# Which units of layer 0's MLP carry a modulation block's sums and transposes

## The reference

```python
def modulation(cvec, w, b):
    m = jax.nn.silu(cvec) @ w + b
    return jnp.split(m[..., None, :], 6, axis=-1)

def sq_relu_mlp(h, w1, w2):
    return jnp.square(jax.nn.relu(h @ w1)) @ w2

for i in range(DEPTH_2):
    sh1, sc1, g1, sh2, sc2, g2 = modulation(c, w_mod[i], b_mod[i])
    csh1, csc1, cg1, csh2, csc2, cg2 = modulation(c_ctx, w_mod[i], b_mod[i])
    ...
    x = sublayer_residual(x, sq_relu_mlp(x * (1.0 + sc2) + sh2, mlp_w1[i], mlp_w2[i]), g2, ln_g[i, 1], ln_b[i, 1])
    if not last:
        ...
        xc = sublayer_residual(xc, sq_relu_mlp(xc * (1.0 + csc2) + csh2, mlp_w1[i], mlp_w2[i]), cg2, ln_g[i, 1], ln_b[i, 1])
```

## Time and profile before

| what | value |
|---|---|
| median of 3 runs | 1266.71 us (1266.68 to 1266.92) |
| the profiled execution | 1269.88 us |
| its span, first to last instruction | 1268.1 us |
| mean granted clock of PE | 0.996 |
| PE busy | 1237.6 us, 98% |
| DVE busy | 886.8 us, 70% |
| ACT busy | 571.9 us, 45% |
| DMA | 218.44 MB, mean 172 GB/s |
| chain that ended last | PE 86%, DVE 4%, ACT 4%, DMA 3% |

### The profile page before, as it was taken

The page is one execution under the profiler, slowest core; times in us unless marked ns, Lnnn a source line. Parts: engine busy times, 40 slices in busy tenths (PEclk is TensorE's granted clock), DMA queues, the critical chain, the costliest instruction groups (busy, mean ns, idle before and its releaser), DMA issues.

```text
span 1268.1 us, 23901 instructions
## 1 busy us (share of the span) xinstructions
PE 1237.6 (98%) x10201; PEld 1150.3 (91%) x10201; DVE 886.8 (70%) x1381; ACT 571.9 (45%) x894; POOL 97.5 (8%) x144
## 2 busy tenths in 40 slices
PE   7999999999999999999999999999999999899997
PEld 4899999999988788999998998998999779899997
DVE  4667765677664675678686787786887987767656
ACT  4443346645774454545413313223155665634531
POOL 0111112100001111000000011111100000000000
PEclk9999999999999999999999999999999999999998
DMA  9997898546344554222545456576444203555550
GB/s 353 393 305 242 269 251 198 158 159 196 97 159 159 183 178 155 101 74 93 167 151 166 126 174 196 175 244 199 133 134 155 79 2 131 169 199 180 187 167 34
DMA packets 170283, 218.44 MB, mean 172 GB/s; under 512 B 6224, under 2 KB 147993, under 8 KB 170042
## 3 DMA queue, kind: packets, MB, share of 16 engines
q1 hardware_dynamic: 140328, 148.18, 35.6%
q0 software_dynamic: 29152, 67.42, 17.5%
q10 hardware_dynamic: 698, 1.32, 0.3%
HBM read 215.77 MB, written 1.12 MB: 171 GB/s over the span
## 4 chain that ended last, share of the span: by engine, by line
PE 86%; DVE 4%; ACT 4%; DMA 3%; issue 2%; SPq 1%; POOL 0%; DVEq 0%; ACTq 0%
PE bank L1401 31%; PE bank L723 13%; PE bank L742 10%; PE bank L775 7%; PE bank L758 4%; PE bank L1295 2%; PE bank L1368 1%; DMA raw<-in_w_in 1%; PE bank L1382 1%; PE bank L833 1%; SPq L570 1%; PE bank L1558 1%; ACT whi L1630 1%; PE bank L1496 1%; DMA pre<-in_w_ada 1%
## 5 line engine op out<-in xcount | busy, mean ns | idle before, releaser
L2251 DVE TENSOR_TENSOR wlo<-raw,whi 128x2048 fp32r<-128x2048 f32 x131 | 297.3, 2274 | 87.5 <-ACT whi L1630 87.1
L1630 ACT ACTIVATE whi<-raw 128x2048 fp32r<-128x2048 f32 x131 | 247.9, 1899 | 182.5 <-PE bank L1401 129.6
L1401 PE MATMUL bank<-a_lo,whi 128*128 128x256 f32 (+1 forms) x656 | 159.4, 314 | 0.0
L1401 PE MATMUL bank<-whi,m_hi 128*128 128x256 f32 x528 | 148.0, 280 | 0.0
L1401 PE MATMUL bank<-whi,m_lo 128*128 128x256 f32 x528 | 147.7, 280 | 0.0
L1401 PE MATMUL bank<-wlo,m_hi 128*128 128x256 f32 x528 | 147.7, 280 | 0.0
L1401 PEld LDWEIGHTS bank<-a_lo,whi 128*128 128x128 f32 x656 | 107.0, 188 | 8.8
L723 PE MATMUL bank<-h_hi,whi 128*128 128x256 f32 x368 | 104.2, 283 | 0.0
L723 PE MATMUL bank<-h_lo,whi 128*128 128x256 f32 x368 | 102.5, 278 | 0.0
L723 PE MATMUL bank<-h_hi,wlo 128*128 128x256 f32 x368 | 102.4, 278 | 0.0
L1401 PEld LDWEIGHTS bank<-whi,m_lo 128*128 128x128 f32 x528 | 100.3, 190 | 0.0
(11 more groups left out here) (476 smaller groups left out, 3314.3 us busy)
## 6 DMA issues: line engine op xcount, KB each, us to landing
raw<-in_mlp_w SPq DMA_DIRECT2D x64, 1024.0 KB, 5.2
raw<-in_w_in SPq DMA_DIRECT2D x32, 1024.0 KB, 7.7
graw_b<-in_w_mod POOLq DMA_DIRECT2D x64, 512.0 KB, 5.1
raw<-in_ev_w_in SPq DMA_DIRECT2D x12, 1024.0 KB, 5.1
pre<-in_w_ada SPq DMA_DIRECT2D x16, 512.0 KB, 9.7
graw_a<-in_w_mod POOLq DMA_DIRECT2D x16, 512.0 KB, 6.8
Y<-in_w_mod POOLq DMA_DIRECT2D x16, 512.0 KB, 4.1
raw<-in_od_w_qkv SPq DMA_DIRECT2D x6, 1024.0 KB, 4.8
```

Source lines behind the costliest of these rows:

```text
L1401: mm = nc.tensor.matmul(o, x, y, start=(k == 0 and i == 0), stop=(k == KT - 1 and i == 2))
L1630: nc.scalar.activation(split_pair(u, kt * cols)[0], landing(u, kt * cols), ACT.Copy).then_inc(hi_done, 1)
L2251: nc.vector.tensor_tensor(split_pair(u, n)[1], landing(u, n), bf(whi[u % HI], n), ALU.subtract).then_inc(lo_done, 1)
```

## The change

Two tables in the kernel's plan are edited. In round 1, the quarters of the units j = 0 to 7 go from 1, 1, 1, 0, 2, 1, 2, 2 to 2, 2, 2, 0, 1, 1, 1, 1; the sum stays ten. Block 19 is turned after unit (1,0) instead of (1,1), block 20 after (1,2) instead of (1,5). Block 21, the fourth, is still turned after (1,7), and its four quarters are in one slot each. Nothing else is changed.

```diff
--- before.py
+++ after.py
@@ -422,13 +422,13 @@
         GY_BANK = (7, 0, 7, 6)
         KV_OUT = 10
         U_Q, B_LOOP, LRING = 72, 18, 3
-        LOOP_N = [[0, 0, 0, 0, 1, 1, 2, 2], [1, 1, 1, 0, 2, 1, 2, 2], [3, 2, 1, 1, 3, 3, 3, 3], [3, 2, 1, 1, 2, 2, 2, 0]]
+        LOOP_N = [[0, 0, 0, 0, 1, 1, 2, 2], [2, 2, 2, 0, 1, 1, 1, 1], [3, 2, 1, 1, 3, 3, 3, 3], [3, 2, 1, 1, 2, 2, 2, 0]]
         LOOP_Q, n_ = {}, 0
         for r_ in range(4):
             for j_ in range(8):
                 LOOP_Q[r_, j_] = range(n_, n_ + LOOP_N[r_][j_])
                 n_ += LOOP_N[r_][j_]
-        REDUCE = {(0, 6): 18, (1, 1): 19, (1, 5): 20, (1, 7): 21, (2, 2): 22, (2, 4): 23, (2, 6): 24, (2, 7): 25,
+        REDUCE = {(0, 6): 18, (1, 0): 19, (1, 2): 20, (1, 7): 21, (2, 2): 22, (2, 4): 23, (2, 6): 24, (2, 7): 25,
                   (3, 1): 26, (3, 2): 27, (3, 5): 28, (3, 7): 29}
         LN_CALL = [0, 2, 4, 5]
         LN_T0 = [24, 32, 40, 48, 56]
```

## The result

| | before | changed |
|---|---|---|
| median, 8 runs each | 1266.91 us (1266.01 to 1270.23) | 1270.38 us (1269.71 to 1271.80) |
| ratio of the medians | | 1.0028, 95% interval 1.0019 to 1.0037 |
| the profiled execution | 1269.88 us | 1271.80 us |
| its span | 1268.1 us | 1270.0 us |
| PE busy | 1237.6 us | 1237.1 us |

The account below looks back on a forecast made before the run. PE, busy for 98% of the span, was taken to bound the kernel. A wait of +2.6, a clock fall of +1.7 and closer spacing of -1.1 gave +3.2 us on 1266.7: 1269.9 us, range 1267.8 to 1271.8.

Parts of the forecast that it names:

- the wait: Behind (1,2), PE waits for DVE's sums before block 20's transposes: 2.6 us, bounds 0.5 and 3.5.
- the spacing: Closer matmuls in (1,1), (1,6) and (1,7): 0.2 + 0.9 = 1.1 us gained; other bound 0.9 lost.
- No second wait: In (1,4), DVE has the last `m_lo` of (1,3) by 719.8, so PE doesn't wait again.
- Steps 1 to 3: DVE in slots (1,0) to (1,2): on time, then 2.8 us late, then PE waits 2.6 us for its sums.
- the lighter slots pay nothing: DVE's slots (1,4), (1,6) and (1,7) are lighter by 2.65 us each, but nothing waited for them: no gain.
- The clock term: Behind the new wait after (1,2), the granted clock falls for a few us: 1.7 us lost.
- the wait comes but the clock stays: Rival: wait behind (1,2) without the clock's fall, 1268.2 us, or 1269.3 without closer spacing; chance 0.27.
- The 0.2 us for (1,1): In (1,1), closer spacing of matmuls gains 2% of 11 us, 0.2 us.

Follow-up runs that it names:

- e9: The kernel before again, unedited, a single execution: 1269.76 us.
- e4: The kernel before with only block 19 moved, turned after (1,0), round 1 summing 2, 0, 1, 0, 2, 1, 2, 2 quarters: ratio 0.9995, 1267.41 us.
- e6: The kernel before, in round 0 of layer 1's MLP the weight split behind unit j = 2 put behind the tile of j = 3: ratio 0.9986, 1267.23 us.
- e1: The changed kernel with block 20 turned after (1,3) instead of (1,2): ratio 0.9997 to the kernel before, 1268.19 us.
- e2: The changed kernel with DVE's quarters in slot (1,2) ahead of its weight split: ratio 0.9994 to the kernel before, 1267.11 us.
- e8: The changed kernel with both reorderings, those of e2 and e6: ratio 0.9978 to the kernel before, 1265.76 us.
- e5: The changed kernel with the split of slot (1,2) between its two quarters: ratio 1.0004 to the kernel before, 1268.65 us.
- e7: The changed kernel again, unedited, on the second chip: ratio 1.0026 to the kernel before, 1271.97 us.
- e10: The changed kernel again, unedited, a single execution: 1269.74 us.
- e12: The changed kernel again, unedited, a single execution: 1274.29 us.
- e3: The changed kernel with three more DVE operations of 128x512 in slot (1,2) ahead of the quarters: ratio 1.0049 to the kernel before, 1274.36 us.
- e11: The kernel of e3 again, a single execution: 1275.02 us.

## Why the prediction was right, point by point

**Where the loss is.** In the first pair of profiles round 1 can be added up. (2,0) starts at 759.41 before and 762.57 after, and (1,0) at 668.08 and 667.98: 3.3 us more. Forecast and found: the wait 2.6 and 2.7; the fallen clock 1.7 and 1.7 ((0.32 + 0.50 + 0.04) x 2); the spacing -1.1 and, from (1,4) to (1,7) without the transposes, 44.5 and 43.5 us, -0.9, with 0.2 more in (1,0). No second wait came behind it.

The same stretch, from the start of (1,0) to that of (2,0), can be read in every trace, and leaves out what differs elsewhere in an execution:

| traces | wait at L1415, us | clock falls behind it | spacing in (1,4) to (1,7) | round 1, us |
|---|---|---|---|---|
| before, e9 | none | no | close, then wide | 91.33, 91.34 |
| e4, e6 | none | no | close, then wide | 90.91, 90.91 |
| e1 | none | no | wide | 91.74 |
| e2, e8 | none | no | close | 90.28, 90.07 |
| e5 | 1.39 | no | close | 91.90 |
| changed: e7, e10 | 2.68, 2.59 | no | close | 92.97, 93.09 |
| changed: first profile | 2.68 | yes | close | 94.59 |
| changed: e12 | 2.68 | yes | wide | 96.24 |
| e3, e11 | 4.76 | yes | wide | 98.49, 98.56 |

The four executions of the changed kernel have a mean of 94.2 us, the three with round 1 as before (before, e9, e6) 91.2. That is 3.0 us, beside 3.5 and 3.3 by the two comparisons of medians.

**Steps 1 to 3** held to within 0.4 us at each row: `sq` at 677.8 and 691.9, found 677.70 and 691.66; split at 697.3, found 697.03; sums done at 704.9, found 704.63; PE there at 702.4, found 702.0. Since both sides came 0.3 to 0.4 us earlier, the wait stayed. e2, e3 and e5 make it a cause and not a neighbour: the wait goes with the time at which DVE ends q11, and the median with the wait. e1 shows the same from PE's side.

**That the lighter slots pay nothing** held: with the wait gone, e1 and e2 are at the kernel before.

**The clock term was put too surely.** The forecast gave the fall of the clock as part of the likeliest case. It fell in two of four executions of the changed kernel with the same wait of 2.6 to 2.7 us, in both with 4.8 us, in one of three with 2.15 us at L1368, and never behind 1.4 to 1.64 us. So its mean share is some 0.85 us, half of 1.7, an estimate from four executions. The rival "the wait comes but the clock stays" isn't another outcome but half of the executions.

**That the sum came so close is in part luck.** The spacing was taken too large as well, and with the other sign: of the 1.1 us forecast, 0.9 are gained in three of four executions, and in the fourth, e12, where (1,4) and (1,5) are wide too, 0.75 are lost (45.2 us against 44.5 before). With 2.7 for the wait, 0.85 for the clock and some -0.5 for the spacing the four traces give the 3.0 us above. The wait is the term that was right, and two errors of 0.6 to 0.9 us largely cancelled.

**The spacing** held as a rule in one direction. With eight transposes ahead of matmuls of 256 columns, the units behind are at the wide spacing in every trace: (1,6) and (1,7) in all four with the turning behind (1,5), (1,4) to (1,7) in e1. Without them, (1,4) to (1,7) are at the close one in the changed kernel three times of four, and in e2, e5 and e8; in e3, e11 and e12 they are wide, each with a fall of the clock just ahead, though the changed kernel's first profile has a fall and close spacing. What decides it there is open. The 0.2 us for (1,1) comes in some executions only. Unit (1,0) was at either spacing, in all 14 traces the one that (0,4) to (0,6) had. Where it was wide and block 19 was turned behind it (e2, e3, e5, e10, e11), (1,1) was close; where it was wide and the turning came behind (1,1) (before, e9), (1,1) was wide too. Where (1,0) was close already, there was nothing to gain.

**Not shown** is the size of the spacing's gain in a median. In the traces it is there: round 1 takes 1.05 us less in e2 than in before, and 0.84 less in e8 than in e6. The medians, e2 (0.9994) and e8 beside e6, agree with it, but don't tell it from nothing. That the moves are worth some 0.9 us once the wait is removed is therefore likely, not settled.

## What to carry to other kernels

When an engine that is always busy gets a wait in its program, work out when the releasing engine gets there, operation by operation, with everything that its slot holds ahead of the release; here a reduction of 1.6 us and one more quarter in the slot before, and one more in the slot itself, turned a wait that had cost nothing into one of 2.7 us. If a step that releases others and one with slack stand in the same slot, put the first ahead: exchanging them in one slot took the whole loss back, and the same kind of repair at another wait was worth 0.14% (0.02 to 0.25%). Before counting on such a repair's full wait, look for what is late next: in e6 it was the split, by 0.6 us. Move the consumer a unit later, if that isn't possible.

## What was not expected of the hardware

The granted clock's fall behind a wait differs from execution to execution: same kernel, same wait of 2.68 us, 0.50 in one and 1.00 in the other. A fall cost 1.6 to 1.7 us, more than half of the wait of 2.7 us that it followed. The Trainium skill ("TensorE: Matmul & The Clock Gate", "What's actually happening") says that the clock gate watches activity in a free-running window, so that the count of slow matmuls at a kernel's start varies from run to run. This case's traces show such a variation behind a wait in mid-kernel: two of four.

Equal matmuls at the same granted clock run at two spacings, 0.113 and 0.118 us for 256 columns, and keep one for tens of microseconds; the changed kernel had units (0,4) to (0,6) at 0.113 us in its first profile and at 0.118 in e10. Single executions of one kernel can differ by this alone by a microsecond or two.
